# A hybrid encoder's attention: native fp32 score and mixing products replaced by three products of high and low parts

## What is computed

```
logits = einsum('bnqhgd,bnkhd->bnhgqk', qb, kb) * HEAD_DIM ** -0.5   # 8 query heads, 2 key/value heads of 128
logits = where(|i - j| <= 128 and in range, logits, -1e30)
probs  = softmax(concat([logits, sink]))[..., :-1]
out    = einsum('bnhgqk,bnkhd->bnqhgd', probs, vb)
```

## Time and profile before

| | us |
|---|---|
| median of 3 runs | 950.02 |
| lowest and highest run | 949.94, 950.05 |
| span of the profiled execution, first to last instruction | 948.2 |
| TensorE matmul busy | 928.1 (98%) |
| VectorE busy | 724.2 (76%) |
| ScalarE busy | 576.6 (61%) |
| DMA | 174.62 MB, 184 GB/s on average |

### The profile page before, as it was taken

How to read it: one execution, slowest core, us unless ns; L and a number is a source line. 1 busy time by engine, 2 the same in 40 slices (tenths; PEclk the granted TensorE clock), 3 DMA queues, 4 the chain that set the end, 5 groups by cost and what they waited for, 6 DMA issues and landing times.

```text
span 948.2 us, 12500 instructions
## 1 busy us (share of the span) xinstructions
PE 928.1 (98%) x5068; PEld 800.5 (84%) x5068; DVE 724.2 (76%) x971; ACT 576.6 (61%) x730; POOL 1.4 (0%) x9
## 2 busy tenths in 40 slices
PE   4999999999999999999999999999999999999996
PEld 3898888988888888888889889888888888888885
DVE  5887898787867867767867688888878676866755
ACT  4578889764356644555345889887435564545540
POOL 0000000000000000000000000000000000000000
PEclk9999999999999999999999999999999999999998
DMA  9546444584485655566453544456756656555621
GB/s 330 159 160 200 135 156 156 185 303 166 156 266 183 200 195 178 194 201 207 157 162 122 204 159 157 132 179 192 261 177 216 229 185 203 189 179 196 202 90 45
DMA packets 118457, 174.62 MB, mean 184 GB/s; under 512 B 3968, under 2 KB 78976, under 8 KB 117888
## 3 DMA queue, kind: packets, MB, share of 16 engines
q1 hardware_dynamic: 118256, 173.79, 55.1%
q10 hardware_dynamic: 144, 0.03, 0.0%
HBM read 172.76 MB, written 1.05 MB: 183 GB/s over the span
## 4 chain that ended last, share of the span: by engine, by line
PE 97%; DVE 1%; DMA 1%; ACT 0%; SPq 0%; issue 0%; DVEq 0%
PE ring L541 16%; PE ring L543 16%; PE ring L542 16%; PE ring L594 9%; PE ring L590 9%; PE ring L593 5%; PE ring L591 5%; PE misc L543 5%; PE misc L541 5%; PE misc L542 4%; PE misc L771 2%; PE misc L809 1%; PE misc L829 1%; PE ring L714 1%; DMA sb_hb<-in_w_in_dram 1%; PE ring L725 1%
## 5 line engine op out<-in xcount | busy, mean ns | idle before, releaser
L1245 DVE TENSOR_TENSOR sb_w_lo<-sb_raw,sb_w_hi 128x2048 fp32r<-128x2048 f32 x138 | 294.7, 2148 | 67.5 <-ACT sb_w_hi L925 67.4
L925 ACT CAST sb_w_hi<-sb_raw 128x2048 fp32r<-128x2048 f32 x138 | 246.2, 1795 | 16.1 <-DMA sb_raw<-in_w_proj_rnn_dram 3.9
L541 PE MATMUL ring<-sb_w_hi,sb_x_both 128*128 128x512 f32 x272 | 108.1, 397 | 0.0
L594 PE MATMUL ring<-sb_x_both,sb_w_hi 128*128 128x512 f32 x272 | 107.6, 396 | 0.0
L590 PE MATMUL ring<-sb_x_both,sb_w_hi 128*128 128x512 f32 x272 | 107.5, 395 | 0.0
L543 PE MATMUL ring<-sb_w_hi,sb_x_both 128*128 128x512 f32 x272 | 106.1, 390 | 0.0
L542 PE MATMUL ring<-sb_w_lo,sb_x_both 128*128 128x512 f32 x272 | 106.0, 390 | 0.0
L593 PE MATMUL ring<-sb_x_both,sb_w_lo 128*128 128x256 f32 x272 | 75.7, 278 | 0.0
L591 PE MATMUL ring<-sb_x_both,sb_w_lo 128*128 128x256 f32 x272 | 75.4, 277 | 0.0
L541 PE MATMUL ring<-sb_x_both,sb_w_hi 128*128 128x256 f32 x256 | 73.0, 285 | 0.0
L543 PE MATMUL ring<-sb_x_both,sb_w_lo 128*128 128x256 f32 x256 | 72.4, 283 | 0.0
(11 more groups left out here) (223 smaller groups left out, 2085.8 us busy)
## 6 DMA issues: line engine op xcount, KB each, us to landing
sb_raw<-in_w_in_dram SPq DMA_DIRECT2D x40, 1024.0 KB, 5.2
sb_raw<-in_w_up_dram SPq DMA_DIRECT2D x34, 1024.0 KB, 5.2
sb_raw<-in_w_down_dram SPq DMA_DIRECT2D x18, 1024.0 KB, 4.9
sb_raw<-in_w_proj_attn_dram SPq DMA_DIRECT2D x8, 1024.0 KB, 5.0
sb_raw<-in_w_proj_rnn_dram SPq DMA_DIRECT2D x8, 1024.0 KB, 5.1
sb_hb<-in_w_up_dram SPq DMA_DIRECT2D x8, 1024.0 KB, 5.2
sb_raw<-in_w_out_dram SPq DMA_DIRECT2D x6, 1024.0 KB, 6.0
sb_raw<-in_w_ple_gate_dram SPq DMA_DIRECT2D x6, 1024.0 KB, 5.7
```

The source lines that it names most:

```text
L541: nc.tensor.matmul(dst, lhs[0], rhs[0], start=first, stop=False)
L594: last = nc.tensor.matmul(bank_of(*key), hi[:, cols], x_both[:, k + 1], start=False, stop=k + 2 == KT)
L925: nc.scalar.copy(hi_at[home][:, at], raw_at[home][:, at]).then_inc(s_hi_part, 1)
L1245: nc.vector.tensor_tensor(lo_at[home][:, 0:size], raw_at[home][:, 0:size], hi_at[home][:, 0:size].bitcast(F32), ALU.subtract).then_inc(s_s ...
```

## The change

Scores and mixing go through `three`, and their operands get low parts. `qkT` becomes fp32r (ScalarE's copy rounds), `pT` is written as `p_hi`, a copy of `v` as `v_hi`. VectorE makes the low parts: five of queries and keys (`qk_lo`, 128x512 each, PSUM minus SBUF; queries into `a_lo`, keys into places of `a_hi` that are written later), one of `v` (`v_low`, 128x512), and in each round one of the turned probabilities (`probs_low`, 128x1024, PSUM minus SBUF, into the place of the first four heads of `qkT`). Waits follow: the fifth turn and the first scores wait for the fourth `qk_lo` where they waited for ScalarE's copy, `turn_probs` of round 0 and the scores of round 2 for the fifth, `mix_values` for `probs_low` and for `v`. The first `probs_low` of a layer also waits for round 1 of the scores.

```diff
+        v_hi = again("v_hi", [P, TT, KV_HEADS, HEAD_DIM], F32R, at + 4 * KT * SEQ)
+        v_lo = again("v_lo", [P, TT, KV_HEADS, HEAD_DIM], F32R, at)
+        qkT, at = sb_at("qkT", [P, QK_HEADS, SEQ], F32R)
+        p_lo = again("p_lo", [P, TT, GROUP, P], F32R, at)
+        p_hi = again("p_hi", [P, TT, GROUP, P], F32R, at)
...
+        def qk_lo_of(pair):
+            first = 2 * pair
+            if first < HEADS:
+                return a_lo[:, first:first + 2, :]
+            return a_hi[:, 0:HEADS, :].rearrange("p (g i) s -> p g i s", g=KV_HEADS)[:, :, 0, :]
...
                     if i == 4:
-                        pe.wait_ge(s_qk_ready, value("qk_ready", l, 4))
+                        pe.wait_ge(s_qk_lo_ready, value("qk_lo_ready", l, 4))
...
                 if r == 0:
-                    pe.wait_ge(s_qk_ready, value("qk_ready", l, 4))
+                    pe.wait_ge(s_qk_lo_ready, value("qk_lo_ready", l, 4))
...
+                keys = [qkT[:, HEADS + g, :], a_hi[:, GROUP * g, :]]
                 for i in range(GROUP):
-                    last = nc.tensor.matmul(misc[:, i // 2, SEQ * (i % 2):SEQ * (i % 2 + 1)],
-                                            qkT[:, GROUP * g + i, b * P:(b + 1) * P], qkT[:, HEADS + g, :],
-                                            start=True, stop=True)
+                    head = GROUP * g + i
+                    last = three(misc[:, i // 2, SEQ * (i % 2):SEQ * (i % 2 + 1)],
+                                 [x[:, head, b * P:(b + 1) * P] for x in (qkT, a_lo)], keys, True, True)
...
-                pe.wait_ge(s_probs_back, value("probs_back", l, r + 1))
+                pe.wait_ge(s_v_ready, value("v_ready", l, 1))
+                pe.wait_ge(s_probs_lo, value("probs_lo", l, r + 1))
                 for kb in range(TT):
-                    last = nc.tensor.matmul(misc[:, 2, :], v[:, kb, r // TT, :], pT[:, kb, :, :],
-                                            start=kb == 0, stop=kb == TT - 1)
+                    last = three(misc[:, 2, :], [x[:, kb, r // TT, :] for x in (v_hi, v_lo)],
+                                 [p_hi[:, kb, :, :], p_lo[:, kb, :, :]], kb == 0, kb == TT - 1)
...
                     if name == "ga0":
                         qk_copies(l, [4])
+                        all_emptied(act, l, [("kv", t) for t in range(TT)])
+                        nc.scalar.copy(v_hi[:, :, :, :].rearrange("p t h d -> p (t h d)"),
+                                       v[:, :, :, :].rearrange("p t h d -> p (t h d)")).then_inc(s_v_hi, 1)
...
+            def qk_lo(l, steps):
+
+                for i in steps:
+                    dve.wait_ge(s_qk_ready, value("qk_ready", l, i + 1))
+                    pair = QK_PAIRS[i]
+                    nc.vector.tensor_tensor(qk_lo_of(pair), misc[:, min(i, 3), :].rearrange("p (h s) -> p h s", h=2),
+                                            qkT[:, 2 * pair:2 * pair + 2, :].bitcast(F32),
+                                            ALU.subtract).then_inc(s_qk_lo_ready, 1)
...
+            def v_low(l):
+                dve.wait_ge(s_v_hi, value("v_hi", l, 1))
+                nc.vector.tensor_tensor(v_lo[:, :, :, :].rearrange("p t h d -> p (t h d)"),
+                                        v[:, :, :, :].rearrange("p t h d -> p (t h d)"),
+                                        v_hi[:, :, :, :].rearrange("p t h d -> p (t h d)").bitcast(F32),
+                                        ALU.subtract).then_inc(s_v_ready, 1)
+
+            def probs_low(l, r):
+
+                dve.wait_ge(s_probs_back, value("probs_back", l, r + 1))
+                if r == 0:
+                    dve.wait_ge(s_scores, value("scores", l, TT))
+                nc.vector.tensor_tensor(p_lo[:, :, :, :].rearrange("p a g t -> p (a g t)"),
+                                        misc[:, 2:4, :].rearrange("p a n -> p (a n)"),
+                                        p_hi[:, :, :, :].rearrange("p a g t -> p (a g t)").bitcast(F32),
+                                        ALU.subtract).then_inc(s_probs_lo, 1)
...
                     split_to(l, f"rg{i // RNN_BLOCKS}", i % RNN_BLOCKS)
+                    if name == "ga0":
+                        qk_lo(l, range(4))
                     gate_input(l, i)
                     split_to(l, name, 1)
                     if i + 2 < 2 * RNN_BLOCKS:
                         conv(l, i + 2)
+                    if name == "ga0":
+                        qk_lo(l, [4])
+                    if i == 3:
+                        v_low(l)
+                    if 3 <= i <= 6:
+                        probs_low(l, i - 3)
                     if 2 <= i <= 5:
                         softmax_max(l, i - 2)
```

More of the change, by code:

```diff
@@ L238 @@
 PER = dict(
-    ln_step=2 * TT * LN_STEPS, ln_norm=4 * TT, x_turned=3 * 4, x_hi=3 * 4, x_ready=3 * 4,
+    qk_lo_ready=5, probs_lo=ROUNDS, v_ready=1, v_hi=1, ln_step=2 * TT * LN_STEPS, ln_norm=4 * TT, x_turned=3 * 4, x_hi=3 * 4, x_ready=3 * 4,
     rope_step=6, qk_turned=5, qk_ready=5,
@@ L284, in hybrid_encoder @@
         lnp = sb("lnp", [P, 2, D])
-        qk = sb("qk", [P, TT, QK_HEADS, HEAD_DIM])
-        v = sb("v", [P, TT, KV_HEADS, HEAD_DIM])
-        qkT = sb("qkT", [P, QK_HEADS, SEQ])
+        qk, at = sb_at("qk", [P, TT, QK_HEADS, HEAD_DIM])
+        v_hi = again("v_hi", [P, TT, KV_HEADS, HEAD_DIM], F32R, at + 4 * KT * SEQ)
+        v, at = sb_at("v", [P, TT, KV_HEADS, HEAD_DIM])
+        v_lo = again("v_lo", [P, TT, KV_HEADS, HEAD_DIM], F32R, at)
+        qkT, at = sb_at("qkT", [P, QK_HEADS, SEQ], F32R)
+        p_lo = again("p_lo", [P, TT, GROUP, P], F32R, at)
         yg = qk[:, :, :, :].rearrange("p t h d -> p (t h d)")[:, 0:KT * SEQ].rearrange(
@@ L296, in hybrid_encoder @@
         soft = sb("soft", [P, GROUP, SEQ])
-        pT = sb("pT", [P, TT, GROUP, P])
+        pT, at = sb_at("pT", [P, TT, GROUP, P])
+        p_hi = again("p_hi", [P, TT, GROUP, P], F32R, at)
         scan_in, at = sb_at("scan_in", [P, 2, 4, SEQ])
@@ L347, in hybrid_encoder @@
         s_qk_ready = sem("qk_ready")
+        s_qk_lo_ready = sem("qk_lo_ready")
         s_scores = sem("scores")
@@ L353, in hybrid_encoder @@
         s_probs_back = sem("probs_back")
+        s_probs_lo = sem("probs_lo")
+        s_v_hi = sem("v_hi")
+        s_v_ready = sem("v_ready")
         s_mixed = sem("mixed")
@@ L802, in scores @@
                 if r == 0:
-                    pe.wait_ge(s_qk_ready, value("qk_ready", l, 4))
+                    pe.wait_ge(s_qk_lo_ready, value("qk_lo_ready", l, 4))
                 else:
                     if r == TT:
-                        pe.wait_ge(s_qk_ready, value("qk_ready", l, 5))
+                        pe.wait_ge(s_qk_lo_ready, value("qk_lo_ready", l, 5))
                     pe.wait_ge(s_exp_done, value("exp_done", l, 5 * r))
+                keys = [qkT[:, HEADS + g, :], a_hi[:, GROUP * g, :]]
                 for i in range(GROUP):
-                    last = nc.tensor.matmul(misc[:, i // 2, SEQ * (i % 2):SEQ * (i % 2 + 1)],
-                                            qkT[:, GROUP * g + i, b * P:(b + 1) * P], qkT[:, HEADS + g, :],
-                                            start=True, stop=True)
+                    head = GROUP * g + i
+                    last = three(misc[:, i // 2, SEQ * (i % 2):SEQ * (i % 2 + 1)],
+                                 [x[:, head, b * P:(b + 1) * P] for x in (qkT, a_lo)], keys, True, True)
                 last.then_inc(s_scores, 1)
@@ L1029, in probs_back @@
                 act.wait_ge(s_probs_turned, value("probs_turned", l, r + 1))
-                nc.scalar.copy(pT[:, :, :, :].rearrange("p a g t -> p (a g t)"),
+                nc.scalar.copy(p_hi[:, :, :, :].rearrange("p a g t -> p (a g t)"),
                                misc[:, 2:4, :].rearrange("p a n -> p (a n)")).then_inc(s_probs_back, 1)
```

## The result

| | before | after |
|---|---|---|
| median, 8 runs each | 950.03 us | 952.9 us |
| lowest and highest | 949.94, 951.14 | 952.83, 953.15 |
| span of the profiled execution | 948.2 us | 951.1 us |

The ratio is 1.0027, with a 95% interval of 1.0018 to 1.0035: 0.27% slower. 952.3 was predicted, 0.24% slower. The profiled execution after took 953.0 us, so 1.9 us lie around its span, 1.8 in the working of before.

The account below looks back on a forecast made before the run. TensorE's matmul queue was taken as the bound. Per layer, 2.56 us saved against about 3.7 of waits and refills gives +1.15; two layers +2.3, so 948.2 + 2.3 + 1.8 = 952.3 us, range 948.2 to 954.8.

Parts of the forecast that it names:

- What TensorE saves: Score rounds shrink from 1.73 to 1.44 us and mixes from 1.72 to 1.37; 5.1 us over eight rounds.
- the bound of 1.36: Upper limit for a 128x1024 low part out of PSUM; its range costs 0 to 0.66 us a layer, to 953.6.
- VectorE becomes the bound: Rival: slow 128x1024 pieces or PSUM readers make VectorE's 3.1 lateness at turn 3 reach the end; 953.6 to 955, chance 0.14.
- Step 1: Last turn of queries waits for the fourth `qk_lo`; TensorE 1.76 us late, 1.47 after round 0 of the scores.
- Step 2: VectorE's 2.4 us of room absorbs four `qk_lo`; the fifth makes the maxima 0.6 late, with no wait at `turn_probs`.
- Steps 3 to 6: Mix 0 waits 0.5 us for `probs_low`, turn 1 ties, mix 1 waits 0.9, mix 2 doesn't wait, TensorE 1.35 late.
- the first tie: At turn 1 `attn_out`'s low part was due at 130.1 and TensorE at 130.2; no wait was counted.
- Step 7: At turn 3 round 2's low part and TensorE both come at 166.3, a tie worth 0 to 0.3; mix 3 gains 0.35.
- the balance: Per layer: 2.56 us saved, about 3.7 of waits and refills (1.76 + 0.7 + 1.1 + 0.15), so +1.15.
- only the first wait counts: Rival: `probs_low` hides and only the fifth turn's 1.76 wait costs; 948.4 us, -0.17%, chance 0.20.
- The low parts hide altogether: Rival: no low part makes TensorE wait, so all 5.1 us are won; 944.9 us, chance 0.12 including a partial form.
- The fall of the clock: Rival: after a wait TensorE drops to 1.2 GHz, costing 5.5 us more, twice; 963 us, chance 0.02.

Follow-up runs that it names:

- e11: Changed kernel with one more unread 128x1024 VectorE instruction a layer, just ahead of round 2's `probs_low` and so of turn 3; 956.26 us.
- e5: Changed kernel with the first four `qk_lo` moved earlier in VectorE's queue, right behind the first weight split of ga0's step; 954.01 us.
- e6: Changed kernel with `v_low` and `probs_low` moved ahead of VectorE's convolution; 953.55 us.
- e4: Changed kernel cut to the mix: three products and low parts for values and probabilities only, scores native; 951.88 us.
- e1: Changed kernel without any low parts; the three passes read the high parts again and wait only for what they waited for before; 946.1 us.
- e10: Changed kernel with scores only, mix native, first four `qk_lo` behind the first weight split, the fifth behind the first maxima; 947.73 us.
- e2: Changed kernel with all low parts made and waited for, but native products on the rounded operands; 955.83 us.
- e3: Changed kernel cut to the scores: three products and low parts of queries and keys only, mix native; 951.4 us.
- e9: Changed kernel with the low parts of the gates' weights made by GpSimd and not by VectorE; 963.07 us.

## Why the prediction was right

By its own steps; all latenesses are less the 0.08 us by which layer 1 starts later in the trace after (86.67 against 86.59).

- **What TensorE saves.** Twelve score passes took 1.43 us (96.25 to 97.68 in the chain), 1.44 predicted; six of the mix 1.39 (173.39 to 174.78), 1.37 predicted. Right.
- **The cost of the pieces.** `qk_lo` comes every 0.60 us, `probs_low` is 1.22 long with 1.13 to the next instruction, out of PSUM as out of SBUF. The value taken, 1.14, was right; the bound of 1.36 was not touched, and with it the condition of the rival *VectorE becomes the bound* falls. What that rival said of the end, one for one with VectorE's lateness at turn 3, is nevertheless what e11 measured: turn 3 starts when VectorE is done.
- **Step 1.** The fifth turn ends at 96.25 (95.59 + 0.66), 1.76 late as predicted.
- **Step 2.** The maxima start at 101.86 against 101.17: 0.6 late. No wait at turn 0.
- **Steps 3 to 6.** Mix 0 waits 0.61 (0.5 predicted). Turn 1, the first tie, shows no wait, but its turns start 0.19 behind the pass before them (130.12 to 130.31) instead of 0.12 and take 0.82 instead of the 0.80 of e5: 0.1, where 0 was taken. Mix 1 waits 0.69 (0.9 predicted), since VectorE is 1.8 late there (137.58 against 135.71) and not 1.95: by the prediction's own numbers 2.35 less 0.46 is 1.9. Mix 2 doesn't wait and starts 1.73 late (1.7 predicted).
- **Step 7, the term that was mis-sized.** VectorE ends the low part of round 2 at 165.75 + 0.68 = 166.43, 0.08 of it offset: 166.35 where 166.3 was predicted. TensorE left mix 2 1.40 late (1.35 predicted), so it would have been ready at 164.92 + 1.40 = 166.32. But a tie was not worth the mean of 0 and 0.3, the 0.15 of the balance. The turns started 0.14 behind their releaser ("issue" in the chain), and the step to the next pass took 0.82 us (166.58 to 167.40) instead of 0.79. From 1.40 late at the end of mix 2, TensorE became 1.77 late: 0.37, where 0.15 was taken. That is 0.22 of the 0.28 missing in a layer; the rest is 0.05 from upstream.

The sum made of waits came out right since it followed VectorE's lateness from wait to wait. Read as a list of separate costs it would mislead: e5 and e6 show that a wait taken out of that list is paid at the next. The prediction's sentence that ties may fall either way by 0.3 was wrong: both ties fell on the dear side, by 0.1 at turn 1 and 0.37 at turn 3, and so did the one at turn 3 of e4 (0.12).

Of the rivals, "only the first wait counts" fell with the waits at both mixes. "The low parts hide altogether" had 944.9 for its price; e1, where they don't exist, measured 946.1, so even that price was too good, in the ruler by 2 x 0.43 for the bank that ScalarE empties. The fall of the clock didn't come in this kernel, but did in e5.

Open: what a piece ahead of VectorE's last wait would cost, how much of e5's excess is the clock, and whether the mix alone, reordered as the scores were in e10, would gain.

## What to carry to other kernels

Where one engine waits for another at some point, find the last place ahead of it where the other engine still waits itself, and count its work from there: a piece put in between costs its full length (1.14 us gave 1.15), one behind the point nothing. Work further ahead first fills the engine's own waits (7.0 us of low parts made VectorE 3.2 late). And a wait that is removed returns at the next while that queue is as long as before. A saving on the engine that waits is partly turned into more waiting (e2: 1.6 of 2.56 us). So split such a change, keep the half whose price fits into the spare time (e10: scores alone, 0.25% faster), and put its pieces where they are needed. And book a tie at its dear side.

## What was not expected of the hardware

**The clock after one wait.** In e5 TensorE rested for 2.35 us ahead of mix 0. The table by stretches, with the granted clock behind the five engines, and then the chain:

```profile
118.00:122.00 4.00, 1.77 (x6) 1.51 (x7) 3.93 (x6) 3.99 (x4) 0.00 (x0) 0.90 0.64 193
122.00:124.00 2.00, 2.00 (x11) 1.93 (x10) 1.88 (x6) 1.81 (x7) 0.00 (x0) 0.50 0.37 142
124.00:128.00 4.00, 4.00 (x33) 4.00 (x33) 4.00 (x2) 4.00 (x12) 0.00 (x0) 0.92 0.13 13
```

```profile
120.23 0.47 PE misc L555
...
121.84 0.43 PE misc L557
122.27 0.21 PE ring L555
...
124.61 0.19 PE ring L557
124.80 0.12 PE ring L555
```

From 121.4 to 124.7 us, beginning 1.2 us after TensorE had started again, the passes are slow; in the stretch that lies wholly inside, the granted clock is 0.50, 1.2 GHz, and passes of 512 columns take 0.43 us instead of 0.23, those of 256 columns 0.21 instead of 0.12. After waits of up to 1.56 us (the kernel after, e3, e6, e11) it stayed at 1.00. The prediction priced such a fall at 5.5 us each; here it took about 2 x 0.20 + 12 x 0.09 = 1.5 us, and the wait at mix 1 (0.69 in the kernel after) swallows part of it: mix 1 starts at 139.60 instead of 138.96, and turn 3 at 167.12 instead of 166.58. That is the 0.5 of its ruler. Not all of e5's time is explained so: one of its five runs had a mean granted clock of 0.998, that of the kernel before, and still took 953.63. The Trainium skill, "TensorE: Matmul & The Clock Gate", HAM oscillation, names idle gaps as what brings the half clock back; the trace of e5 agrees in kind.

A gap of that length doesn't always do it. In e9 TensorE waits 2.44 us at layer 1's fifth turn and the clock falls (the first line), and 2.35 us at its turn 3, up to 170.92, and it doesn't (the second). The same turn 3 in layer 2, after 2.36 us, is followed by 0.50 again (641 to 644 us).

```profile
98.00:100.00 2.00, 2.00 (x9) 1.81 (x8) 2.00 (x2) 2.00 (x5) 0.00 (x0) 0.50 0.00 0
171.00:180.00 9.00, 9.00 (x71) 8.74 (x72) 7.35 (x7) 4.63 (x6) 0.00 (x0) 1.00 0.34 108
```

**GpSimd beside VectorE.** In e9 a subtraction of 128x1024 took GpSimd 3.16 us on average (VectorE 1.22), and VectorE's instructions beside it stretched. The group of GpSimd's, and one of its instructions:

```profile
L557 POOL TENSOR_TENSOR sb_w_lo<-sb_raw,sb_w_hi 128x1024 fp32r<-128x1024 f32 x16 | 50.6, 3164 | 584.3 <-ACT sb_w_hi L954 584.3
```

```profile
127.54 3.70 POOL L557 TENSOR_TENSOR sb_w_lo<-sb_raw,sb_w_hi 128x1024 fp32r<-128x1024 f32 x1 [15.93 <-ACT sb_w_hi L954]
```

VectorE's instruction beside one that GpSimd ran from 108.67 on for 2.94 us, and the one beside the piece above:

```profile
110.10 2.07 DVE L1544 SCALAR_TENSOR_TENSOR sb_lnp<-sb_tmp 128x512 f32<-128x512 f32 x1 [0.75 <-ACT sb_tmp L1016]
...
128.90 2.37 DVE L1485 TENSOR_TENSOR sb_sm<-sb_sm 128x4 f32<-128x4 f32 x1
```

The first is 0.69 us long in the kernel before and the second, of four columns, 0.16. All five of GpSimd's pieces in layer 1's stretch have such a neighbour, which loses 1.4 to 2.2 us, more than the 1.14 that VectorE gives up. The second ends at 131.27, 0.03 behind GpSimd's piece (131.24), and the first 0.56 behind it, a little less than its own length, as if neither had moved on before GpSimd was done. GpSimd's piece of 3.70 began beside a split of VectorE's that kept its ordinary 2.27 us; the shortest of the five took 2.40. The Trainium skill, "GPSIMD Engine Reference", Specifications, says that GpSimd shares its SBUF interfaces with VectorE and that instructions of VectorE with two SBUF inputs contend; this trace agrees, and all five stretched instructions have two such inputs.
